# Weight sums of the seven-product networks: VectorE adds in place, or accumulating transfers into DRAM scratch

## The chip, the cores and the metric

The kernel runs on one core of one Trainium2 chip. The metric is the device time of one execution in microseconds; the time before is the median of three executions.

## What is computed

Two transformer blocks in a row on 512 tokens of width 1024, in float32. The parts that the change touches are the three feed-forward networks:

```
u = relu(rms_norm(h) @ mlp_w1);  h = h + (u * u) @ mlp_w2            # mlp: 1024 -> 4096 -> 1024
x = x + 0.5 * (silu(n @ w1) * (n @ w3)) @ w2                          # ffn1 and ffn2: 1024 -> 2816 -> 1024
```

Everything else (a mixer of forgetting attention and gated linear attention, cross attention to a memory of 256 rows, differential attention, a sparse attention, the projections) is as it was.

## The kernel before

Each float32 factor is split into a high and a low part, and a product is three matmuls (high by high, high by low, low by high). Weights come from DRAM into `raw` (two panels of 1024 rows by 256 columns, 1 MB each), ScalarE makes the high part (`wh`), VectorE the low part (`wl`), and TensorE multiplies. A panel p is loaded once `conv_done` says that panel p-2 has been converted; it is converted once TensorE has read panel p-2 out of `wh` and `wl`. The loads are issued in program order on SP's queue, whose waits stand in front of them.

Part of each network's first layer is done by seven products of half-size blocks in place of eight (a Winograd form of Strassen's scheme), in phases: three for mlp, two each for ffn1 and ffn2. A phase has groups: two for each mlp phase, four for each ffn phase, 22 groups in all. A group multiplies a 2 by 2 arrangement of 512x256 weight blocks, A11 and A12 (from `one`) and A21 and A22 (from `two`), with token blocks that are ready in SBUF. Its seven left factors are A11, A12, A22 and four sums: S3 = A11 + A21, S1 = A21 + A22, S2 = S3 + A22, S4 = A12 + S2 (the signs lie in the token blocks). A block's number of conversion is its place in A11, A12, A22, S3, S1, S2, S4. TensorE takes them as A11, A12, S2, S3, S1, A22, S4; from the second group on, S4 of the group before stands after A11 of the next (`in_turn`). Converted blocks go round six slots (`RING = 6`), so conversion n of a phase waits until product n-5 is done.

Four blocks are loaded for a group (`group_loads`, the transfer is L630), 512 KB each, into four buffers BP, BZ, BQ, BR. The buffers are those of `raw` or, for every other group, a spare area (`xl_f`, for ffn2 `al_f`). A11 lies in BP, A21 in BZ, A12 in BQ, A22 in BR. When VectorE has made the low part of A11, it adds in place (`add_up`, L3022): `sum_3` makes S3 in BP, `sum_1` makes S1 in BZ, `sum_2` makes S2 in BR after the low part of A22, `sum_4` makes S4 in BQ after the low part of A12. ScalarE's `block_high` (L2055) turns a block into its high part; for A11 it waits until all three of A11, A12 and A22 have landed. VectorE's `block_low` (its line in the profile is L2499, that of the helper `low`) makes the low part. ScalarE's `kept` (L2062) takes a product out of PSUM; TensorE's products S2, S1 and A22 wait for the first, second and third of a group. GpSimd has no work in the kernel.

Of the kernel before, what the change touches and what calls it, by code (L numbers as in the profile page):

```python
# [5 lines left out]
ALU = mybir.AluOpType  # L6
# [134 lines left out]


RING = 6
BP, BZ, BQ, BR = range(4)
BUF = {A11: BP, A12: BQ, A22: BR, S3: BP, S1: BZ, S2: BR, S4: BQ}
SUM = {S3: 1, S1: 2, S2: 3, S4: 4}


def net_of(g):
# [23 lines left out]
    return 12 * NETS.index(name) + 7 * PHASES[name, 1][0] + 3 * m + n  # L173


def sum_count(g, n):

    return 20 * (net_of(g) + 1) + 4 * g + n


def token_count(name, m, n):

    return 20 * NETS.index(name) + 4 * PHASES[name, 1][0] + 5 * m + n


def buffers(g):
# [89 lines left out]
def build(nc, d, out):  # L276
    ctx = ExitStack()
    with ctx:
# [118 lines left out]
        out_t, out_d = sem("out_t"), sem("out_d")  # L397
        out_c = [sem("out_c" + str(half)) for half in range(2)]
        st_z, st_r = ([sem(f"st_{b}{n}") for n in range(2)] for b in "zr")
        st_h, st_l, st_a, st_q, st_e, st_c = (sem("st_" + n) for n in ("h", "l", "a", "q", "e", "c"))  # L400


# [135 lines left out]
        def weights(g):  # L538
# [3 lines left out]
                return tuple(mw1[:, :, r * D + (2 * i + e) * PC:r * D + (2 * i + e + 1) * PC] for e in range(2))  # L542
            return tuple(w[:, :, (r - 1) * D + i * PC:(r - 1) * D + (i + 1) * PC] for w in ffw[net][0:2])

        def same_buffers(g):

            return [q for q in range(g) if buffers(q) == buffers(g)]
# [5 lines left out]
        def _(sp):  # L553
# [61 lines left out]
            def group_loads(g, p, free):  # L615

                one, two = weights(g)
                before = same_buffers(g)
                for b, src in ((BZ, two[:, 0:HT]), (BP, one[:, 0:HT]), (BQ, one[:, HT:KT]), (BR, two[:, HT:KT])):
                    if before:  # L620
                        q = before[-1]
                        if b in (BP, BR):
                            sp.wait_ge(st_a, sum_count(q, 3 if b == BP else 4))
                        else:
                            sp.wait_ge(st_l, high_count(q, S1 if b == BZ else S4))
                    if buffers(g):
# [3 lines left out]
                    sp.dma_start(raw_of(g, b), src).then_inc((st_r, st_z, st_r, st_r)[b][buffers(g)], 16)  # L630

            def phase(name, r, free, w2):

                g0, n, p = PHASES[name, r]
                for g in range(g0, g0 + n):
                    group_loads(g, p, free)
                last = g0 + n - 2
                for j in range(4):
                    if j == 0:
                        sp.wait_ge(st_l, high_count(last, S1))  # L640
                        sp.wait_ge(st_a, sum_count(last, 3))
# [82 lines left out]
            sp.wait_ge(out_d, 16 * QT)  # L724


        @block.tensor
# [854 lines left out]
        def _(act):  # L1582
# [885 lines left out]
        def _(dve):  # L2468
# [543 lines left out]
            def block_low(g, a):  # L3012

                dve.wait_ge(st_h, high_count(g, a))
                if a in SUM:
                    dve.wait_ge(st_a, sum_count(g, SUM[a]))
                to_h, to_l = parts_of(g, a)
                low(to_l, raw_of(g, BUF[a]), to_h, st_l)

            def add_up(g, to, of):  # L3020

                nc.vector.tensor_tensor(raw_of(g, to), raw_of(g, to), raw_of(g, of), ALU.add).then_inc(st_a, 1)  # L3022

            def sum_3(g):

                dve.wait_ge(st_l, high_count(g, A11))
                dve.wait_ge(st_z[buffers(g)], 16 * len(same_buffers(g)) + 16)
                add_up(g, BP, BZ)

            def sum_1(g):  # L3030

                dve.wait_ge(st_a, sum_count(g, 1))
                add_up(g, BZ, BR)

            def sum_2(g):

                dve.wait_ge(st_l, high_count(g, A22))
                dve.wait_ge(st_a, sum_count(g, 2))
                add_up(g, BR, BP)

            def sum_4(g):

                dve.wait_ge(st_l, high_count(g, A12))
                dve.wait_ge(st_a, sum_count(g, 3))
                add_up(g, BQ, BR)

            def bank(g, at):

# [20 lines left out]
            def first_blocks(g):  # L3069

                def early():
                    block_low(g, A11)
                    block_low(g, A12)

                def later():
                    block_low(g, A22)
                    sum_3(g)
                    sum_1(g)
                    block_low(g, S3)
                    sum_2(g)  # L3080
                return early, later, lambda: block_low(g, S1)

            def mlp_phase(r):

                g0, n, p = PHASES["mlp", r]

                def relu_square(g, buf, c, u):
                    dve.wait_ge(st_c, 3 * g + c)
                    nc.vector.scalar_tensor_tensor(buf, buf, 0.0, buf, ALU.max, ALU.mult).then_inc(ml_e, 1)

                def low_part(k, side, src, count):
                    dve.wait_ge(ml_hi, count)
                    low(al[:, k:k + 2, side], src, ah[:, k:k + 2, side], ml_lo)

                for g in range(g0, g0 + n):
                    k, more = 4 * (g - g0), g + 1 < g0 + n
                    block_low(g, S2)
                    sum_4(g)
# [24 lines left out]
                    relu_square(g, E_ul, 3, 2 * g + 2)  # L3123
                g, k = g0 + n - 1, 4 * (n - 1)
                low_part(k + 2, LEFT, E_ul, made_count(g, 3))
                low_part(k, RIGHT, E_tr, made_count(g, 4))
                conv(p + 1)

            def ffn_phase(name, r, dst):
# [17 lines left out]
                for g in range(g0, g0 + n):  # L3147
                    more = g + 1 < g0 + n
                    block_low(g, S2)
                    sum_4(g)  # L3150
# [5 lines left out]
                    if more:  # L3156
                        block_low(g + 1, A11)
                        block_low(g + 1, A12)
                        block_low(g + 1, A22)
                        sum_3(g + 1)  # L3160
                        sum_1(g + 1)
                    made_22(g)
                    if not more:
                        conv(p)
                    else:
                        block_low(g + 1, S3)
                        sum_2(g + 1)
# [510 lines left out]
```

## Time and profile before

| | |
|---|---|
| median of three executions | 2138.14 us (2136.89 to 2138.54) |
| the profiled execution, its own time | 2138.95 us |
| its span | 2137.2 us |
| TensorE (PE) busy | 2118.8 us, 99% of the span |
| VectorE (DVE) busy | 1372.5 us, 64% |
| ScalarE (ACT) busy | 1032.6 us, 48% |
| GpSimd (POOL) busy | 0.2 us |
| read from HBM, written | 188.73 MB, 2.10 MB |

The span is that of the profiled execution from its first to its last instruction; the 1.75 us around it belong to its own time. All starts are microseconds from the span's start. PE's busy time counts matmuls whose ends are modelled. SPq is SP's queue: its rows show when a transfer was issued, not when it landed.

### The profile page before, as it was taken

The numbers are of one execution on the slowest core, as the hardware profiler recorded it, in microseconds if no ns is written. First come the engines' busy times: TensorE is split into PE (matmuls) and PEld (weight loads), VectorE is DVE, ScalarE is ACT, GpSimd is POOL, SyncE is SP. The second block draws the span as 40 slices with busy tenths as digits, with TensorE's granted clock in tenths as the row PEclk, the third lists the DMA queues.
The fourth block names the chain that finished last, engine by engine and source line by source line (L and its number), as shares of the span: only waits on it lengthen the run. The fifth ranks groups of instructions, "written<-read, shape, count | busy, mean of one in ns | idle before, by whom it ended". The sixth has DMA issues, their size and how long they took to land.

```text
span 2137.2 us, 32530 instructions
## 1 busy us (share of the span) xinstructions
PE 2118.8 (99%) x13100; PEld 1819.8 (85%) x13100; DVE 1372.5 (64%) x2281; ACT 1032.6 (48%) x1738; POOL 0.2 (0%) x4
## 2 busy tenths in 40 slices
PE   9999999999999999999999999999999999999999
PEld 7888988888998988898988888887777888899997
DVE  4664663467664767775856777647776356686674
ACT  6654545543533543453543565546666234354344
POOL 0000000000000000000000000000000000000000
PEclk9999999999999999999999999999999999999999
DMA  5121522133233132424323622321111233242421
GB/s 189 60 80 60 180 97 80 40 99 118 80 119 118 61 98 84 138 75 138 100 80 98 181 83 82 98 84 50 40 37 40 79 99 99 87 139 72 138 68 71
DMA packets 190920, 199.74 MB, mean 93 GB/s; under 512 B 8481, under 2 KB 185778, under 8 KB 190258
## 3 DMA queue, kind: packets, MB, share of 16 engines
q1 hardware_dynamic: 190770, 197.66, 29.2%
q8 instruction: 104, 1.70, 0.3%
q14 instruction: 46, 0.38, 0.1%
HBM read 188.73 MB, written 2.10 MB: 89 GB/s over the span
## 4 chain that ended last, share of the span: by engine, by line
PE 93%; DVE 3%; ACT 2%; issue 1%; DMA 1%; SPq 0%; DVEq 0%; ACTq 0%
PE lin L733 20%; PE lin L735 19%; PE lin L734 19%; PE mix L1279 3%; PE mix L1280 3%; PE mix L1281 3%; PE score L1279 3%; PE score L1280 3%; PE score L1281 3%; PE turned L834 3%; PE score L929 3%; PE mix L943 2%; PE turned L1279 1%; PE turned L1280 1%; PE turned L1281 1%
## 5 line engine op out<-in xcount | busy, mean ns | idle before, releaser
L733 PE MATMUL lin<-xh,wh 128*128 128x512 f32 (+1 forms) x1032 | 407.5, 395 | 1.7 <-DVE wl L2494 1.2
L735 PE MATMUL lin<-xh,wl 128*128 128x512 f32 (+1 forms) x1032 | 394.8, 383 | 0.0
L734 PE MATMUL lin<-xl,wh 128*128 128x512 f32 (+1 forms) x1032 | 393.7, 382 | 0.0
L733 PE MATMUL lin<-ah,wh 128*128 128x512 f32 (+1 forms) x788 | 308.5, 392 | 1.4 <-DVE al L2499 0.6
L735 PE MATMUL lin<-ah,wl 128*128 128x512 f32 (+1 forms) x788 | 306.0, 388 | 0.0
L734 PE MATMUL lin<-al,wh 128*128 128x512 f32 (+1 forms) x788 | 305.9, 388 | 0.0
L2488 DVE TENSOR_TENSOR wl<-raw,wh 128x2048 fp32r<-128x2048 f32 x85 | 194.8, 2292 | 123.7 <-ACT wh L1595 123.7
L733 PEld LDWEIGHTS lin<-xh,wh 128*128 128x128 f32 x1032 | 194.2, 188 | 45.4 <-issue 9.6
L735 PEld LDWEIGHTS lin<-xh,wl 128*128 128x128 f32 x1032 | 194.0, 188 | 39.0
L734 PEld LDWEIGHTS lin<-xl,wh 128*128 128x128 f32 x1032 | 194.5, 188 | 34.8 <-issue 1.0
L1595 ACT ACTIVATE wh<-raw 128x2048 fp32r<-128x2048 f32 x85 | 162.0, 1906 | 113.4 <-PE lin L735 106.4
L733 PEld LDWEIGHTS lin<-ah,wh 128*128 128x128 f32 x788 | 148.0, 188 | 33.2 <-issue 1.6
L735 PEld LDWEIGHTS lin<-ah,wl 128*128 128x128 f32 x788 | 147.9, 188 | 30.7
L734 PEld LDWEIGHTS lin<-al,wh 128*128 128x128 f32 x788 | 148.0, 188 | 30.1 <-issue 0.2
L2494 DVE TENSOR_TENSOR wl<-raw,wh 128x1024 fp32r<-128x1024 f32 x90 | 109.5, 1220 | 40.4 <-ACT wh L1602 39.9
L2602 DVE CUSTOM_DVE_ANT_0 arena<-score,cst 128x128 f32<-128x128 f32 (+2 forms) x224 | 97.6, 486 | 58.0 <-PE score L929 46.6
L1692 ACT ACTIVATE arena<-arena,negm 128x128 f32<-128x128 f32 (+2 forms) x224 | 122.8, 555 | 3.1 <-DVE negm L2602 3.0
L1680 ACT ACTIVATE arena<-turned 128x512 f32<-128x512 f32 (+1 forms) x128 | 68.8, 582 | 112.5 <-PE turned L834 112.2
L1602 ACT ACTIVATE wh<-raw 128x1024 fp32r<-128x1024 f32 x90 | 94.1, 1052 | 36.1 <-PE lin L735 23.8
L1280 PE MATMUL mix<-arena_r,wh 128*128 128x256 f32 x352 | 98.9, 281 | 0.0
L1281 PE MATMUL mix<-arena_r,wl 128*128 128x256 f32 x352 | 98.9, 281 | 0.0
L1279 PE MATMUL mix<-arena_r,wh 128*128 128x256 f32 x352 | 98.9, 281 | 0.0
(434 smaller groups left out, 4301.1 us busy)
## 6 DMA issues: line engine op xcount, KB each, us to landing
raw<-in_w_in_dram SPq DMA_DIRECT2D x38, 1024.0 KB, 5.3
raw<-in_ffn_w_dram SPq DMA_DIRECT2D x28, 1024.0 KB, 5.2
raw<-in_mlp_w_dram SPq DMA_DIRECT2D x20, 1024.0 KB, 5.2
raw<-in_ffn_w_dram SPq DMA_DIRECT2D x32, 512.0 KB, 4.8
raw<-in_xattn_wkv_dram SPq DMA_DIRECT2D x8, 1024.0 KB, 5.3
raw<-in_w_out_dram SPq DMA_DIRECT2D x8, 1024.0 KB, 5.3
xl_f<-in_ffn_w_dram SPq DMA_DIRECT2D x16, 512.0 KB, 6.0
al_f<-in_ffn_w_dram SPq DMA_DIRECT2D x16, 512.0 KB, 5.5
```

The source lines that it names most:

```text
L733: nc.tensor.matmul(o, w[0], x[0], start=first, stop=False)
L734: nc.tensor.matmul(o, w[0], x[1], start=False, stop=False)
L735: return nc.tensor.matmul(o, w[1], x[0], start=False, stop=last)
L1279: nc.tensor.matmul(o[:, c, :], left_h[:, k, cols], XS_h[:, b, k, :], start=begins, stop=False, skip_group_check=True)
L1280: nc.tensor.matmul(o[:, c, :], left_h[:, k, cols], XS_l[:, b, k, :], start=False, stop=False, skip_group_check=True)
L1281: mm = nc.tensor.matmul(o[:, c, :], left_l[:, k, cols], XS_h[:, b, k, :], start=False, stop=k == HT - 1, skip_group_check=True)
L1595: nc.scalar.activation(wh[:, p % 2], raw[:, p % 2], ACT.Copy).then_inc(hi_done, 1)
L1602: nc.scalar.activation(wh[:, p % 2, :, cols], raw[:, p % 2, :, cols], ACT.Copy).then_inc(hi_half[c], 1)
L1692: op = nc.scalar.activation(PB[:, s % 2, a, col:col + nk], SM[:, a, col:col + nk], ACT.Exp, bias=negm[:, at:at + 1], scale=-1.0, accum_out ...
L2488: nc.vector.tensor_tensor(wl[:, p % 2], raw[:, p % 2], wh[:, p % 2].bitcast(F32), ALU.subtract).then_inc(conv_done, 1)
L2494: nc.vector.tensor_tensor(wl[:, p % 2, :, cols], raw[:, p % 2, :, cols], wh[:, p % 2, :, cols].bitcast(F32), ALU.subtract).then_inc(conv_d ...
L2602: op = nc.vector.tensor_tensor_reduce(out=SM[:, a, col:col + nk], in0=ps[a][:, col:col + nk], in1=mask, scale=scale, scalar=BIG, op0=ALU.a ...
```

## The change

The sums are no longer made on VectorE. GpSimd, idle until now, issues transfers from DRAM to DRAM: for each unit eight of them, each waiting for the one before (`su`). A unit is one group of mlp (blocks of 512x256, 512 KB a transfer, six units) or a whole phase of ffn1 or ffn2 (512x1024, 2 MB a transfer, four units). In a unit S3, S1, S2 and S4 are each made by a plain copy and an accumulating transfer (`accum_op=add`) onto it. It starts when TensorE has finished the first five panels.

SP now loads seven blocks for a group: A11, A12 and A22 first; then, once the unit's sums are there, S1 into BZ; S3 into BP when A11's low part is made; S2 into BR when A22's low part is made and S3 and S1 of the group have landed; S4 into BQ. ScalarE waits for the landing of a sum in place of the addition. The waits on `st_a` for sums go.

```diff
-SUM = {S3: 1, S1: 2, S2: 3, S4: 4}
+SUM = {S3: 0, S1: 1, S2: 2, S4: 3}
+UNITS = [(g_, 1, PC) if key_[0] == "mlp" else (g_, n_, n_ * PC) ...]
+        block_sums = [nc.dram_tensor(f"block_sums{u}", (4, HT * PART, width), F32, kind="Internal").ap() ...]
...
             def group_loads(g, p, free):
...
+                load(BP, one[:, 0:HT], st_r, S3, None)
+                load(BQ, one[:, HT:KT], st_r, S4, None)
+                load(BR, two[:, HT:KT], st_r, S2, None)
+                sp.wait_ge(su, 128 * (u + 1))
+                load(BZ, made(S1), st_z, S1, None)
+                load(BP, made(S3), st_z, None, A11)
+                sp.wait_ge(st_z[n], 64 * len(before) + 32)
+                load(BR, made(S2), st_z, None, A22)
+                load(BQ, made(S4), st_z, None, A12)
...
+        @block.gpsimd
+        def _(pool):
+            def step(n, dst, src, **kw):
+                if n:
+                    pool.wait_ge(su, 16 * n)
+                pool.dma_start(dst, src, **kw).then_inc(su, 16)
+            pool.wait_ge(lin_done, 2 * SUMS_FROM)
+            for u, (g, n, width) in enumerate(UNITS):
...
+                step(8 * u, s3, a11)
+                step(8 * u + 1, s3, a21, accum_op=ALU.add)
+                step(8 * u + 2, s1, a21)
+                step(8 * u + 3, s1, a22, accum_op=ALU.add)
+                step(8 * u + 4, s2, s3)
+                step(8 * u + 5, s2, a22, accum_op=ALU.add)
+                step(8 * u + 6, s4, s2)
+                step(8 * u + 7, s4, a12, accum_op=ALU.add)
...
-                    act.wait_ge(st_a, sum_count(g, SUM[a]))
+                    act.wait_ge(st_z[buffers(g)], 64 * len(same_buffers(g)) + (32 if a in (S1, S3) else 64))
...
-                        sum_3(g + 1)
-                        sum_1(g + 1)
...
-                        sum_2(g + 1)
```

The helper `load` in `group_loads` waits, in this order, for the buffer's last user in the group before that had the same buffers, for the low part of the block that the sum replaces, and for what the old code waited for (`conv_done` or `lin_done`), and then issues one transfer.

## Rows read from the trace of the kernel before

**Rows 1.** The page: busy times, and SP's DMA queue.

```profile
PE 2118.8 (99%) x13100; PEld 1819.8 (85%) x13100; DVE 1372.5 (64%) x2281; ACT 1032.6 (48%) x1738; POOL 0.2 (0%) x4
...
q1 hardware_dynamic: 190770, 197.66, 29.2%
```

**Rows 2.** Waits of PE: who waited for what: us in total, times, longest.

```profile
PE score L1279 <- DVE wl L2499: 1.2, 2, 0.8
```

**Rows 3.** Windows: busy us of each engine, clock, DMA share, GB/s.

```profile
240.00:320.00 80.00, 79.72 (x461) 70.40 (x460) 46.75 (x48) 34.46 (x48) 0.00 (x0) 1.00 0.43 145
...
540.00:580.00 40.00, 40.00 (x317) 39.00 (x315) 29.00 (x32) 23.59 (x31) 0.00 (x0) 1.00 0.21 70
```

**Rows 4.** Groups of instructions by line: VectorE's sums.

```profile
L3022 DVE TENSOR_TENSOR raw<-raw 128x1024 f32<-128x1024 f32 x44 | 53.7, 1219 | 0.4
...
L3022 DVE TENSOR_TENSOR xl_f<-xl_f 128x1024 f32<-128x1024 f32 x28 | 34.2, 1220 | 0.2
...
L3022 DVE TENSOR_TENSOR al_f<-al_f 128x1024 f32<-128x1024 f32 x16 | 19.5, 1220 | 0.1
```

**Rows 5.** First products of the mlp phases: min/median/max ns, first and last start.

```profile
L1279 PE MATMUL score<-arena_r,xh x24: 277/281/284, 534.4 to 556.9; 128*128 128x256 f32 x24
...
L1279 PE MATMUL score<-arena_r,wh x24: 277/281/283, 540.1 to 551.2; 128*128 128x256 f32 x24
...
L1279 PE MATMUL score<-arena_r,xh x24: 277/281/284, 617.9 to 640.3; 128*128 128x256 f32 x24
...
L1279 PE MATMUL score<-arena_r,xh x24: 277/281/284, 701.3 to 723.7; 128*128 128x256 f32 x24
```

**Rows 6.** DMA issues by line: KB each, median us to landing.

```profile
raw<-in_w_in_dram SPq DMA_DIRECT2D x38, 1024.0 KB, 5.3
...
raw<-in_ffn_w_dram SPq DMA_DIRECT2D x32, 512.0 KB, 4.8
```

**Rows 7.** L630, the block loads: landing in the window 510 to 523, and in all.

```profile
DMA to landing us min/median/max: 3.9/6.0/8.5
...
DMA to landing us min/median/max: 3.7/5.0/9.8
```

**Rows 8.** PE's timeline when panel 5 starts, and SP's where two networks' block loads start.

```profile
70.28 0.36 PE L733 MATMUL lin<-wh,xh 128*128 128x256 f32 x1
...
510.54 7.58 SPq L630 DMA_DIRECT2D raw<-in_mlp_w_dram  x4
...
864.10 9.08 SPq L630 DMA_DIRECT2D raw<-in_ffn_w_dram  x4
```

**Rows 9.** DVE's timeline, first mlp phase: low parts of A11 and A22.

```profile
524.35 1.22 DVE L2499 TENSOR_TENSOR xh<-raw,xh 128x1024 fp32r<-128x1024 f32 x1
...
529.79 1.22 DVE L2499 TENSOR_TENSOR wl<-raw,wh 128x1024 fp32r<-128x1024 f32 x1
```

**Rows 10.** ACT's timeline, same phase: A11 of the second group, then `kept`.

```profile
540.68 1.04 ACT L2055 ACTIVATE wh<-xl_f 128x1024 fp32r<-128x1024 f32 x1
542.66 0.63 ACT L2080 ACTIVATE arena<-arena 128x512 f32<-128x512 f32 x1 [0.94 <-DVE arena L3055]
...
543.87 0.58 ACT L2062 ACTIVATE arena<-score 128x512 f32<-128x512 f32 x1
```

**Rows 11.** Timelines of DVE, ACT and PE, first group of ffn1.

```profile
878.99 1.22 DVE L2499 TENSOR_TENSOR xh<-raw,xh 128x1024 fp32r<-128x1024 f32 x1 [2.26 <-ACT xh L2055]
...
887.79 1.06 ACT L2055 ACTIVATE wh<-raw 128x1024 fp32r<-128x1024 f32 x1 [1.21 <-DVE raw L3022]
...
890.67 0.39 PE L1279 MATMUL score<-arena_r,wh 128*128 128x256 f32 x1 [0.81 <-DVE wl L2499]
```

**Rows 12.** Second group of ffn1: DVE's low part of A11, ACT's high part of S2.

```profile
894.62 1.22 DVE L2499 TENSOR_TENSOR wl<-xl_f,wh 128x1024 fp32r<-128x1024 f32 x1
...
905.13 1.06 ACT L2055 ACTIVATE wh<-xl_f 128x1024 fp32r<-128x1024 f32 x1 [1.75 <-PE mix L1281]
```

**Rows 13.** ACT's timeline in the panels of the memory's keys and values.

```profile
234.85 1.06 ACT L1602 ACTIVATE wh<-raw 128x1024 fp32r<-128x1024 f32 x1 [2.98 <-DMA raw<-in_xattn_wkv_dram]
```

More of the change, by code:

```diff
@@ L143 @@
 RING = 6
+SUMS_FROM = P0["fv"]
 BP, BZ, BQ, BR = range(4)
 BUF = {A11: BP, A12: BQ, A22: BR, S3: BP, S1: BZ, S2: BR, S4: BQ}
-SUM = {S3: 1, S1: 2, S2: 3, S4: 4}
+SUM = {S3: 0, S1: 1, S2: 2, S4: 3}
+UNITS = [(g_, 1, PC) if key_[0] == "mlp" else (g_, n_, n_ * PC) for key_, (g0_, n_, _) in PHASES.items()
+         for g_ in range(g0_, g0_ + n_, 1 if key_[0] == "mlp" else n_)]
+UNIT_OF = {g_: u_ for u_, (g0_, n_, _) in enumerate(UNITS) for g_ in range(g0_, g0_ + n_)}
 def net_of(g):
@@ L173, in part_count @@
     return 12 * NETS.index(name) + 7 * PHASES[name, 1][0] + 3 * m + n
-def sum_count(g, n):
-    return 20 * (net_of(g) + 1) + 4 * g + n
 def token_count(name, m, n):
-    return 20 * NETS.index(name) + 4 * PHASES[name, 1][0] + 5 * m + n
+    return 20 * NETS.index(name) + 5 * m + n
 def buffers(g):
@@ L399, in build @@
         st_z, st_r = ([sem(f"st_{b}{n}") for n in range(2)] for b in "zr")
+        su = sem("su")
         st_h, st_l, st_a, st_q, st_e, st_c = (sem("st_" + n) for n in ("h", "l", "a", "q", "e", "c"))
@@ L543, in weights @@
             return tuple(w[:, :, (r - 1) * D + i * PC:(r - 1) * D + (i + 1) * PC] for w in ffw[net][0:2])
+        block_sums = [nc.dram_tensor(f"block_sums{u}", (4, HT * PART, width), F32, kind="Internal").ap() for u, (_, _, width) in enumerate(UNITS)]
         def same_buffers(g):
@@ L617, in group_loads, with load @@
                 one, two = weights(g)
[L618 to L626, printed above, removed]
+                before, n = same_buffers(g), buffers(g)
+                u = UNIT_OF[g]
+                at = (g - UNITS[u][0]) * PC
+                def load(b, src, signal, last, extracted):
+                    if last is not None and before:
+                        sp.wait_ge(st_l, high_count(before[-1], last))
+                    if extracted is not None:
+                        sp.wait_ge(st_l, high_count(g, extracted))
+                    if n:
                         sp.wait_ge(lin_done, 2 * free)
@@ L629, in group_loads, with made @@
                         sp.wait_ge(conv_done, p - 1 + b // 2)
-                    sp.dma_start(raw_of(g, b), src).then_inc((st_r, st_z, st_r, st_r)[b][buffers(g)], 16)
+                    sp.dma_start(raw_of(g, b), src).then_inc(signal[n], 16)
+                def made(a):
+                    return tiles(block_sums[u][SUM[a]])[:, :, at:at + PC]
+                load(BP, one[:, 0:HT], st_r, S3, None)
[7 more added lines that the diff above has]
+                load(BQ, made(S4), st_z, None, A12)
             def phase(name, r, free, w2):
@@ L640, in phase @@
                         sp.wait_ge(st_l, high_count(last, S1))
-                        sp.wait_ge(st_a, sum_count(last, 3))
                     elif j == 1:
@@ L724, in _ @@
             sp.wait_ge(out_d, 16 * QT)
+        @block.gpsimd
+        def _(pool):
+            def step(n, dst, src, **kw):
+                if n:
+                    pool.wait_ge(su, 16 * n)
+                pool.dma_start(dst, src, **kw).then_inc(su, 16)
+            pool.wait_ge(lin_done, 2 * SUMS_FROM)
+            for u, (g, n, width) in enumerate(UNITS):
+                (net, r), i = PHASE_OF[g]
+                if net == "mlp":
+                    at = r * D + 2 * i * PC
+                    a11, a12 = (mw1[:, ks, at:at + PC] for ks in (slice(0, HT), slice(HT, KT)))
+                    a21, a22 = (mw1[:, ks, at + PC:at + 2 * PC] for ks in (slice(0, HT), slice(HT, KT)))
+                else:
+                    (a11, a12), (a21, a22) = ([w[:, ks, (r - 1) * D:r * D] for ks in (slice(0, HT), slice(HT, KT))] for w in ffw[net][0:2])
+                s3, s1, s2, s4 = (tiles(block_sums[u][k]) for k in range(4))
+                step(8 * u, s3, a11)
[6 more added lines that the diff above has]
+                step(8 * u + 7, s4, a12, accum_op=ALU.add)
         @block.tensor
@@ L3014, in block_low @@
                 dve.wait_ge(st_h, high_count(g, a))
-                if a in SUM:
-                    dve.wait_ge(st_a, sum_count(g, SUM[a]))
                 to_h, to_l = parts_of(g, a)
                 low(to_l, raw_of(g, BUF[a]), to_h, st_l)
[L3020 to L3045, printed above, removed]
             def bank(g, at):
@@ L3076, in later @@
                     block_low(g, A22)
-                    sum_3(g)
-                    sum_1(g)
                     block_low(g, S3)
-                    sum_2(g)
                 return early, later, lambda: block_low(g, S1)
@@ L3097, in mlp_phase @@
                     block_low(g, S2)
-                    sum_4(g)
                     if g > g0:
@@ L3149, in ffn_phase @@
                     block_low(g, S2)
-                    sum_4(g)
                     if g > g0:
@@ L3159, in ffn_phase @@
                         block_low(g + 1, A22)
-                        sum_3(g + 1)
-                        sum_1(g + 1)
                     made_22(g)
@@ L3166, in ffn_phase @@
                         block_low(g + 1, S3)
-                        sum_2(g + 1)
                         block_low(g + 1, S1)
```

## The prediction

> **What bounds the kernel now.** I read the page first: TensorE is busy 2118.8 of 2137.2 us, the two converting engines 64% and 48%, and GpSimd does nothing [rows 1]. So work taken from VectorE is worth only the time that PE waits for VectorE. The windows put a place to that: in the first mlp phase PE is busy 40.00 of 40.00 us at the full clock [rows 3]. The waits of PE say the same: in all networks it waits for a converted block that the sums delay twice, 1.2 us in total, 0.8 the longest [rows 2]. The third view is the timelines of the first group of a phase and of the second, on every engine, for the slack of each block [rows 5, 9 to 12]; the last is the DMA views, since the change is mostly transfers [rows 1, 6, 7].
>
> The reader is to see a kernel that PE sets. A product of a group takes (540.1 - 534.4) / 2 = 2.85 us [rows 5], so a group 20 us; every deadline below is a product's start.
>
> **What is removed.** The 44 + 28 + 16 = 88 sums at 1.22 us are 107 us of VectorE [rows 4], beside a busy PE. They can give back at most the 1.2 us of [rows 2], and that only if S2 comes no later than now.
>
> **What a transfer costs.** SP's queue moved 197.66 MB in 190770 packets in 29.2% of 16 engines' span [rows 1]: 52 ns for 1036 bytes, 317 GB/s over 16 engines. 512 KB is 1.65 us of that. The shortest landing of such a block is 3.7 and 3.9 us [rows 7], take L = 3.8, so 2.2 us are fixed. That gives 5.5 us for 1 MB (the row has 5.3 [rows 6]), and 8.8 us for 2 MB.
>
> **The chain of sums on GpSimd.** No row shows an accumulating transfer or one from DRAM to DRAM. For the copies I take the same 3.8 and 8.8 us. An accumulate reads two streams and writes one. From below it costs what a copy does; from above I allow four times the data time. I take twice: 5.5 us and 15.4 us. The six mlp units are then 6 x 4 x (3.8 + 5.5) = 223 us, the four ffn units 4 x 4 x (8.8 + 15.4) = 387 us, together 610 us. They start when five panels are done, at 70 us [rows 8], and end at 680 us. By the lower bound they end at 70 + 48 x 3.8 + 32 x 8.8 = 534 us, by the upper (8.8 and 28.6 us for an accumulate) at 970 us. The first unit is wanted about 518 us and done after 37, and ffn1's first at 864 us [rows 8] is done at 70 + 223 + 97 = 390: SP's wait on `su` costs nothing.
>
> The Trainium skill (DMA: Bandwidth & Descriptors, Anatomy of one DMA) gives about 2.0 us plus the bytes over 436 GB/s for a transfer issued from GpSimd. By it the 48 small and 32 large steps would be some 154 + 218 = 372 us, an estimate from the page, and no traffic would be left when the networks begin. Its fixed part agrees with the 2.2 us above.
>
> **The new chain of loads, with idle DMA engines.** S3 and S2 are now two landings in a row behind A11's low part. In ffn1's first group that low part ends at 878.99 + 1.22 = 880.2; plus 2L is 887.8, and S2's high part starts at 887.79 today [rows 11]. No change. In the second group it ends at 895.84 [rows 12]. S2 of that group is product 9 of the phase and S2 of the first, product 2, starts at 890.67 [rows 11], so it is wanted at 910.6 and, with 1.06 + 1.22 us of conversion and 0.2 of handing over, landed by 908.1: 2L may be 12.2, and L 6.1. In the first group of an mlp phase A11's low part ends at 525.6 and A22's at 531.0 [rows 9]; S2 is issued at 531.1, lands at 534.9 and is wanted in SBUF by 540.1 - 2.5 = 537.6. So at L = 3.8 no product waits.
>
> **The queue on SP.** The next group's A11, A12 and A22 are now issued behind S2 and S4 of this one, and ScalarE's A11 waits for all three. In an mlp phase that is five blocks from 531.1: 2.2 + 5 x 1.65 = 10.5 us, 541.6. Behind the waiting A11 stands `kept`: A11's high part, two steps and `kept` itself are about 2.8 us [rows 10], and S1's product, the fifth, wants it at 534.4 + 4 x 2.85 = 545.8. So A11 must have landed by 543.0: 1.4 us to spare, no cost alone.
>
> **Beside GpSimd's transfers** it is no longer free. If the chain of sums runs until 680 us, it covers the mlp phases that start at 534.4 and 617.9, and not the third at 701.3 [rows 5]. Then its 2 MB steps move data (6.6 + 13.2) / 24.2 = 82% of the time. If the two queues share the engines evenly meanwhile, the loads go at 1 - 0.41 = 0.59 of their rate. The five blocks take 2.2 + 8.2 / 0.59 = 16.1 us, land at 547.2, and PE waits 4.2 us for `kept`. S2 of the first group has L = 5.0 on the mean and fits; entirely beside accumulates, at a third of the rate, L is 7.1 and S2 comes 2.3 us late; I take 1 us. That is 5 us a phase, 10 in two.
>
> The Trainium skill (DMA: Bandwidth & Descriptors, Queues, rings and completion order) says that an engine goes round its queues packet by packet, and that it doesn't matter which engine issued a transfer; that speaks for this sharing, and with GpSimd's 4 KB rows against SP's 1 KB rows for a worse one. No row of before shows two busy queues.
>
> Earlier, the memory's keys and values are the tightest place: eight panels of 1 MB in 5.7 us of PE each (48 matmuls of 256 columns at 2.85 / 24 us), DMA share 0.43 over that stretch [rows 3], and ScalarE waits 2.98 us for a load with PE still fed [rows 13]. Beside the mlp sums, which move data 53% of the time, the 3.3 us of a load become 4.5; four tight loads make up to 4.8 us, and I take 2 (bounds 0 and 8). Elsewhere a panel has twice the columns, so some 11 us of PE for the same load, and I take nothing. Sum: 10 + 2 = 12 us.
>
> **Rivals.**
> *Slower by shared DMA engines* (the forecast). For it: 48 x 0.52 + 32 x 2.1 = 92 MB written and more than that read, beside 200 MB today, and margins of 1.4 us. From 2 us (one phase touched lightly) up: if the sums run until 970 us they cover the three mlp phases and ffn1's first and perhaps second, and at a third of the rate the five blocks take 2.2 + 24.8 = 27 us, 15 too many, with 2.3 for S2; five times 17, plus 8, is 93 us.
>
> *The networks don't notice* (not slower). The chain of sums ends before 534 us, as it does if an accumulate costs a copy, or the engines serve both queues without loss. Then nothing waits: 2138 us, within 2 us. It decides at an end of the chain before 534 us, or at L under 5.4 us with A11 landing within 12 us. Against it: an accumulate must read twice. The skill's sum above would give this.
>
> *The sums are late.* SP waits on `su` in the networks, and everything behind it in SP's queue. For mlp that begins when a 512 KB step takes over (701 - 70) / 48 = 13.1 us on the mean. With 28 us for an accumulate and 3.8 for a copy the mean is 16, the last mlp unit comes at 838 in place of 701, and the time is some 137 us more, 2275 us; slower still is open above. Against it: 13.1 is over three times the landing of such a block.
>
> *Faster.* S2 comes earlier with VectorE free and both waits of [rows 2] go: 1.2 us, 2137 us, which a measurement can't tell. For more, VectorE would have to slow PE in a way that no wait shows.
>
> **How the numbers follow.** Contention slows it: 0.54, of which a tenth stays under 0.2%. Unnoticed: 0.27. Late: 0.13. Faster or a small other gain: 0.06, of which half is over 0.2%. About 0.2%, 4 us, is what a measurement of this kernel tells from no change. So slower 0.54 x 0.9 + 0.13 = 0.62, faster 0.03, the same the rest, 0.35. The sum stands against the profiled execution's 2138.95 us, 0.8 over the median: 2138 + 12 = 2150 us. The likeliest case alone has 2140 to 2231. The range takes in the unnoticed case below, 2136, and the heavier contention above and a mild lateness, to 2225; the rest of lateness and of gains stays out.
>
> **What would show it.** Right: rows L3022 gone; VectorE's busy time down by some 107 us; a queue of GpSimd with 80 transfers from 70 us on, ending near 680; PE waits at L1279, released by ACT `kept` (L2062) or by a low part, in the first two mlp phases and in neither of the later networks; landings of block loads over 5 us before the end of the sums and 3.8 after. Wrong: the chain of sums ending before 534 us with PE as busy as before in the phases; or SP waiting on `su` past 701 us, with idle stretches of PE of tens of us ahead of a phase. Waits in ffn2, where no sums run any more, would say that my 2L chain or the order of the queue was mis-sized, not the sharing.

## The result and the profile after

| | before | after |
|---|---|---|
| median | 2137.83 us | 2215.36 us (2212.23 to 2219.13) |
| ratio of the two, interval | | 1.0364 [1.0346, 1.0382] |
| span of the profiled execution | 2137.2 us | 2213.3 us |

The change costs some 77 us; 12 were forecast. The page of the changed kernel, against [rows 1] (its L1322 is L1279 of before, L2542 is L2499, L2105 is L2062, L633 is L630):

```profile
PE 2129.8 (96%) x13100; PEld 1829.4 (83%) x13100; DVE 1280.8 (58%) x2193; ACT 1028.8 (46%) x1738; POOL 81.1 (4%) x84
...
q1 hardware_dynamic: 225618, 232.27, 33.0%
q0 software_dynamic: 33024, 92.28, 17.7%
...
block_sums<-in_ffn_w_dram POOLq DMA_DIRECT2D x24, 2048.0 KB, 14.5
...
block_sums<-in_mlp_w_dram POOLq DMA_DIRECT2D x36, 512.0 KB, 6.8
block_sums<-block_sums POOLq DMA_DIRECT2D x8, 2048.0 KB, 10.2
```

VectorE has 88 instructions fewer and 91.7 us less to do, not the 107 of the prediction: that sum took each addition's whole duration, and in the rows of VectorE neighbouring instructions overlap by about 0.1 us at either end. (Without traffic, in experiment 12, it is 92.7 us, so the transfers have no part in it.) Of the last three rows the first two mix copies and accumulates. PE has as many matmuls as before, and yet is busy 11.0 us longer. Its waits, against [rows 2] (us in total, times, longest):

```profile
PE score L1322 <- DVE wl L2542: 46.0, 5, 16.6
PE mix L1322 <- DVE wl L2542: 16.1, 3, 7.7
...
PE lin L776 <- DVE wl L2531: 1.9, 1, 1.9
PE lin L776 <- DVE arena L2573: 1.7, 1, 1.7
```

The first two rows, 62.1 us where [rows 2] had 1.2, are the networks. PE's timeline puts them into the three mlp phases, 13.73 + 7.68, 13.79 + 6.54 and 16.55 + 1.90 = 60.2 us:

```profile
557.60 0.58 PE L1322 MATMUL score<-arena_r,wh 128*128 128x256 f32 x1 [13.73 <-DVE wl L2542]
...
587.72 0.58 PE L1322 MATMUL mix<-arena_r,wh 128*128 128x256 f32 x1 [7.68 <-DVE wl L2542]
...
667.77 0.58 PE L1322 MATMUL score<-arena_r,wh 128*128 128x256 f32 x1 [13.79 <-DVE wl L2542]
...
777.77 0.58 PE L1322 MATMUL score<-arena_r,wh 128*128 128x256 f32 x1 [16.55 <-DVE wl L2542]
```

The last two rows of the waits are the panels of the memory's keys and values, 3.6 us. So 76.1 us of span are some 61 of waits in the networks, some 3 in those panels, 11 of slower matmuls, and 1 spread elsewhere.

**Which load is late.** The chain that ended last, over the first mlp phase (start, length, what):

```profile
521.18 10.03 DMA raw<-in_mlp_w_dram
531.24 1.07 ACT xh L2098
532.33 1.24 DVE xh L2542
533.58 10.31 DMA raw<-block_sums
...
546.41 13.21 DMA xl_f<-in_mlp_w_dram
...
561.99 10.38 DMA xl_f<-block_sums
...
573.28 12.05 DMA xl_f<-block_sums
```

Read it downwards. A22 takes 10 us to land, and A11's conversion waits for it: A11's low part ends at 533.6, where it ended at 525.6 in the kernel before [rows 9]. PE itself is 3.6 us behind the kernel before at this point (its first product starts at 538.0, not 534.4 [rows 5]), so some 4 us are A22's. Then S3 is issued and takes 10.3 us; S2 is issued behind its landing, a chain that I call the join below. ScalarE's timeline gives the landings, 543.9 for S3 and 555.2 for S2:

```profile
543.92 1.06 ACT L2098 ACTIVATE xh<-raw 128x1024 fp32r<-128x1024 f32 x1 [9.73 <-DMA raw<-block_sums]
...
555.23 1.06 ACT L2098 ACTIVATE wh<-raw 128x1024 fp32r<-128x1024 f32 x1 [9.30 <-DMA raw<-block_sums]
```

So the two landings in a row are 533.6 to 555.2, 21.6 us where 2 x 3.8 were counted, and PE, out of products at 543.9, starts S2's at 557.6. The second group repeats it with S3 at 562.0 and S2 at 573.3.

**Why the landings are long.** Landings of the block loads in the window 500 to 800 us, against [rows 7], what GpSimd's queue moved meanwhile (packets, MB, share of 16 engines), and GpSimd's timeline:

```profile
DMA to landing us min/median/max: 3.9/10.7/15.5
...
q0 software_dynamic: 11308, 44.88, 59.4%
...
518.75 0.76 POOL L748 DMA_DIRECT2D block_sums<-block_sums  x1 [13.53 <-DMA block_sums<-in_ffn_w_dram]
528.18 1.24 POOL L748 DMA_DIRECT2D block_sums<-in_ffn_w_dram  x1 [8.67 <-DMA block_sums<-block_sums]
543.63 0.77 POOL L748 DMA_DIRECT2D block_sums<-block_sums  x1 [14.21 <-DMA block_sums<-in_ffn_w_dram]
...
775.24 1.25 POOL L748 DMA_DIRECT2D block_sums<-in_ffn_w_dram  x1 [11.02 <-DMA block_sums<-block_sums]
```

Here a 2 MB copy takes 9.4 us (518.8 to 528.2) and an accumulate 15.4 (528.2 to 543.6); from one issue to the next the medians of ffn's steps are 10.5 and 15.5 us, and those of mlp's 4.3 and 7.7. The last step begins at 775. SP's S3 of the chain above was issued at 533.6, in the middle of that accumulate. The DMA queues (packets, MB, share of 16 engines) in the windows 533.6 to 536.5, then 537 to 541, then 547 to 552:

```profile
q0 software_dynamic: 152, 0.62, 107.5%
...
q0 software_dynamic: 176, 0.72, 89.9%
q1 hardware_dynamic: 169, 0.17, 15.8%
...
q0 software_dynamic: 404, 1.65, 81.4%
q1 hardware_dynamic: 401, 0.39, 22.6%
```

In the first 2.9 us after the issue not one packet of SP's queue (q1) is recorded; the first starts at 537.1, 3.5 us after the issue. Part of that is there without any other traffic. In the kernel before a load issued at 537.43 has no packet in the 1.00 us from 537.43 to 538.43, and in the next 1.00 us:

```profile
q1 hardware_dynamic: 209, 0.21, 80.6%
```

So 1.0 us is usual and 2.5 us are added. It varies: of the changed kernel's SP loads between 500 and 800 us that were issued with no other load of SP in flight, eleven, the first packet came after 1.0 to 3.8 us, 3.5 in the median. After that the queues take turns, 176 to 169 and 404 to 401 packets, but one of GpSimd's has 4 KB and one of SP's 1 KB: between 547 and 552 us SP gets 0.39 of 2.04 MB, 19%, and 22.6 of the 104.0 points of engine time, 22%. This is turn by turn by packets, not an even share of time. The Trainium skill (DMA: Bandwidth & Descriptors, Queues, rings and completion order) has the engines go round their queues packet by packet; the second and third window agree (176 to 169 and 404 to 401 packets), the 2.5 us added at the start are not in that rule.

**The slower matmuls.** The windows 588 to 594 and 594 to 600 us (busy us and count of each engine, clock, DMA share, GB/s):

```profile
588.00:594.00 6.00, 6.00 (x31) 6.00 (x32) 3.14 (x4) 4.01 (x7) 0.00 (x0) 0.55 1.07 219
594.00:600.00 6.00, 6.00 (x53) 6.00 (x52) 1.57 (x3) 1.79 (x3) 0.00 (x0) 1.00 0.76 151
```

After the 7.68 us in which PE did nothing, the granted clock is 0.55, near its lower level of 1.2 GHz, and 31 matmuls fit into 6 us where 53 fit next. Each of the six waits in the mlp phases, the 1.90 us too, is followed by such a stretch of lower clock; in all the networks' matmuls are busy 11.5 us longer, the rest of PE's work 0.5 us shorter, which makes the 11.0.

### The profile page after: what moved, and what is told of

Same layout as the page of the kernel before. It is cut to its first block, busy times and chain, and to the rows that moved or that the text cites. A ratio compares the mean times of both kernels' runs of the same rounds, so it can differ in the third digit from the quotient of the medians.

```text
span 2213.3 us, 32502 instructions
## 1 busy us (share of the span) xinstructions
PE 2129.8 (96%) x13100; PEld 1829.4 (83%) x13100; DVE 1280.8 (58%) x2193; ACT 1028.8 (46%) x1738; POOL 81.1 (4%) x84
## 3 DMA queue, kind: packets, MB, share of 16 engines
q0 software_dynamic: 33024, 92.28, 17.7%
## 4 chain that ended last, share of the span: by engine, by line
PE 82%; DMA 10%; DVE 4%; ACT 3%; issue 1%; SPq 0%; DVEq 0%; ACTq 0%
PE lin L776 18%; PE lin L778 17%; PE lin L777 17%; PE mix L1322 3%; PE mix L1323 3%; PE mix L1324 3%; DMA xl_f<-block_sums 3%; PE turned L877 3%; PE score L972 3%; DMA raw<-block_sums 2%; PE score L1322 2%; PE mix L986 2%; PE score L1324 2%; PE score L1323 2%; DMA xl_f<-in_mlp_w_dram 2%; DMA raw<-in_mlp_w_dram 1%
## 5 line engine op out<-in xcount | busy, mean ns | idle before, releaser
L776 PEld LDWEIGHTS lin<-xh,wh 128*128 128x128 f32 x1032 | 194.2, 188 | 47.2 <-issue 11.5
L1322 PE MATMUL score<-arena_r,wh 128*128 128x256 f32 x296 | 86.4, 292 | 46.0 <-DVE wl L2542 46.0
L1322 PE MATMUL mix<-arena_r,wh 128*128 128x256 f32 x352 | 101.8, 289 | 16.1 <-DVE wl L2542 16.1
L1323 PE MATMUL mix<-arena_r,wh 128*128 128x256 f32 x352 | 101.3, 288 | 0.0
```

The lines of the kernel that those rows point to most:

```text
L776: nc.tensor.matmul(o, w[0], x[0], start=first, stop=False)
L1322: nc.tensor.matmul(o[:, c, :], left_h[:, k, cols], XS_h[:, b, k, :], start=begins, stop=False, skip_group_check=True)
L1323: nc.tensor.matmul(o[:, c, :], left_h[:, k, cols], XS_l[:, b, k, :], start=False, stop=False, skip_group_check=True)
```

## The experiments

The diffs are against the changed kernel, that of experiment 2 against the kernel before; `...` in a diff stands for lines left out. Ratios are to the kernel before.

**1. No traffic.** GpSimd's transfers go; the order of the loads stays. Weight blocks of the same size are loaded in place of the sums, so the kernel leaves the sums out.

```diff
-                    return tiles(block_sums[u][SUM[a]])[:, :, at:at + PC]
+                    return {S1: two[:, 0:HT], S3: two[:, 0:HT], S2: two[:, HT:KT], S4: one[:, HT:KT]}[a]
-                sp.wait_ge(su, 128 * (u + 1))
-        @block.gpsimd
-            ...
```

> The changed kernel without GpSimd's transfers: SP's seven loads of a group stand in their new order with their new waits, but the four sums are loaded straight from weight blocks of the same size (so the left factors are not the sums), and the wait on su is gone. Theory 1, the shared DMA engines stretch the landings: block loads land in about 3.8 to 5 us again, no wait of PE at L1322-like lines above 1 us, 2137 to 2141 us. Theory 2, the new order of the loads and the two landings in a row cost by themselves: at least 2180 us, with waits of several us in the mlp phases and in ffn1 and ffn2 alike.

2141.48 us, 1.0015 [1.0005, 1.0025]. Landings of block loads between 500 and 800 us:

```profile
DMA to landing us min/median/max: 3.6/4.9/10.1
...
891.21 0.39 PE L1293 MATMUL score<-arena_r,wh 128*128 128x256 f32 x1 [1.64 <-DVE wl L2513]
```

The mlp phases have no wait of PE for a block; PE's timeline shows 1.64 us in ffn1's first group and 1.80 in ffn2's. The traffic is needed for the loss, and the new order by itself costs 3.7 us.

**2. The kernel before, with the traffic for nothing.** GpSimd makes the sums in scratch, VectorE adds as before, nobody reads the scratch.

```diff
+        @block.gpsimd
+            ...  (the 80 steps; sums on VectorE and four loads a group kept)
```

> The kernel before, with its four early loads and the sums on VectorE, and GpSimd's 80 transfers beside it for nothing. Theory 1a, traffic costs only where loads stand late in a chain: 2142 to 2156 us, since A22's late landing (about 10 us in place of 5) still delays S2 by some us in each of three mlp phases. Theory 1b, traffic alone makes the whole loss: 2205 to 2220 us.

2143.30 us, 1.0030 [1.0018, 1.0041].

```profile
DMA to landing us min/median/max: 3.8/11.6/20.9
...
PE score L1313 <- DVE wl L2533: 2.9, 3, 1.7
...
PE lin L767 <- DVE wl L2522: 3.6, 2, 3.0
```

Its landings are as long as in the changed kernel (11.6 against 10.7 us), and it loses 5.5 us. Traffic alone 5.5, order alone 3.7, both 77: the loss comes of the two together, not of either. The old order loads four blocks ahead of any need; the new one issues the sums' loads only when low parts are made and puts two landings of the same group behind each other. Experiment 5 parts these two.

**3. Copies in place of accumulates.** The additions are left out, the steps and the bytes written stay.

```diff
-                step(8 * u + 1, s3, a21, accum_op=ALU.add)
+                step(8 * u + 1, s3, a21)
                 ...
```

> The changed kernel with every accumulating transfer made a plain copy (the sums are then only their last part). The bytes written stay the same, the second stream read goes. If an accumulate costs about twice a copy's data time, the chain of 80 steps ends near 600 us in place of 790, the third mlp phase and perhaps the second have no wait, and the time is 2160 to 2180 us. If accumulates cost what copies do, the chain ends near 790 us as before and the time stays 2210 to 2220 us.

2163.82 us, 1.0125 [1.0109, 1.0140]; q0 has 23808 packets for the same 92.28 MB written, and 12.4%. The accumulates thus bring packets of their own, 9216 of 33024, and 17.7% in place of 12.4% of the engines' span. The landings in the window 510 to 600 us, and GpSimd's last step:

```profile
DMA to landing us min/median/max: 3.8/9.9/14.6
...
628.37 0.74 POOL L748 DMA_DIRECT2D block_sums<-in_ffn_w_dram  x1 [9.17 <-DMA block_sums<-block_sums]
```

While copies of 2 MB run, a block lands in 9.9 us, almost as late as beside copies and accumulates in turn (10.6 in the same window of the changed kernel), and PE's waits in the first mlp phase are 17.4 us against 21.4. What falls is the time for which they run: the chain ends at 638 us in place of 793, the third mlp phase has no wait and the second one of 2.3 us. Most of the difference between 26 us and 77 is that.

**4. All units one group wide.** Steps of 512 KB with 1 KB rows everywhere, 176 steps.

```diff
-UNITS = [(g_, 1, PC) if key_[0] == "mlp" else (g_, n_, n_ * PC) ...]
+UNITS = [(g_, 1, PC) for g_ in range(GROUPS)]
             ...  (and ffn's source blocks a group wide)
```

> The changed kernel with every unit one group wide: ffn1's and ffn2's sums too are made in 512 KB transfers with rows of 1 KB, as many bytes in 176 steps. If the engines take turns packet by packet, the block loads of the mlp phases land in 6 to 8 us in place of 10 to 14 beside rows as short as their own, and PE's waits there fall from 20 us a phase to under 8; the chain runs longer, to about 1000 us, and puts small waits into ffn1: 2160 to 2190 us in all. If the queues share by bytes or time, landings stay at 10 to 14 us, ffn1's phases get waits of 20 us as well, and the time is 2230 us or more.

2162.45 us, 1.0119 [1.0095, 1.0143], landing median 6.4 us between 500 and 800 us; two thirds of the loss gone, although the chain of sums now ends at some 1200 us and touches ffn1, where the longest wait is 5.9 us. It changed three things at once, the rows, the amount of a step, and the length of the chain; 7, 9 and 14 vary the rows and the amount.

**5. S2 need not wait for S3's landing.** S2 and S4 are counted on semaphores of their own.

```diff
-                sp.wait_ge(st_z[n], 64 * len(before) + 32)
-                load(BR, made(S2), st_z, None, A22)
-                load(BQ, made(S4), st_z, None, A12)
+                load(BR, made(S2), st_y, None, A22)
+                load(BQ, made(S4), st_y, None, A12)
             ...  (ScalarE's waits likewise)
```

> The changed kernel with S2 and S4 counted on semaphores of their own, so that S2's load is issued when A22's low part is made and no longer waits until S3 has landed. If the two landings in a row (about 10 us each beside the sums) set the waits of the mlp phases, six groups lose up to 7 us each of their waits, PE keeps its clock for longer, and the time falls by 25 to 45 us, to 2170 to 2190 us. If only the throughput of the shared engines sets them, S3, S2 and what is behind them land when they did before, and the time is 2205 to 2217 us.

2186.76 us, 1.0227 [1.0211, 1.0242]: 28.6 of 77 us back. The other 48 need the traffic and the new order, but not the join. Between 505 and 800 us PE waits 32.1 us, 10.8 of them for `kept`, which the prediction had named:

```profile
560.90 0.55 PE L1322 MATMUL score<-arena_r,wh 128*128 128x256 f32 x1 [7.13 <-ACT arena L2105]
```

**6. The sums pause for mlp.** Nothing is transferred on GpSimd's queue during the mlp phases.

```diff
+PAUSED = {7: P0["ffn1"] - 1, 8: P0["mix2"]}
             ...
+                if u in PAUSED:
+                    pool.wait_ge(lin_done, 2 * PAUSED[u])
```

> The changed kernel with a pause in GpSimd's chain: ffn1's second unit is made from the start of ffn1 on and ffn2's two only when ffn1 is done, so that no sum is being made during an mlp phase. All 80 transfers remain. If it is their time beside the phases that costs, only what the order of the loads alone costs (3.7 us in the run without traffic) and a little of the panels' contention remain: 2140 to 2148 us. If the traffic costs wherever it is, or ffn1's second unit comes late, 2155 us or more.

2170.75 us, 1.0152 [1.0137, 1.0167], where 2140 to 2148 was expected. The mlp phases have no wait left, and their blocks land in 4.8 us in the median. But the two last units now run beside the first panels of the second block's mixer, and PE waits there:

```profile
1166.39 0.66 PE L779 MATMUL lin<-xh,wh 128*128 128x512 f32 x1 [2.63 <-DVE wl L2540]
...
1194.23 0.47 PE L1416 MATMUL score<-wl,ah 128*62 128x256 f32 x1 [2.31 <-DVE wl L2540]
1201.53 0.80 PE L779 MATMUL lin<-xh,wh 128*128 128x512 f32 x1 [3.85 <-DVE wl L2540]
```

**7. The ffn sums in steps of 512 KB, rows of 4 KB kept.** Each step is still waited for before the next. (SP's count of `su` is changed to match.)

```diff
-                if n:
-                    pool.wait_ge(su, 16 * n)
-                pool.dma_start(dst, src, **kw).then_inc(su, 16)
+                for q in range(4) if n >= 48 else (slice(0, 4),):
+                    if made[0]:
+                        pool.wait_ge(su, 16 * made[0])
+                    pool.dma_start(dst[:, q], src[:, q], **kw).then_inc(su, 16)
+                    made[0] += 1
             ...
```

> The changed kernel with ffn's sums made in 512 KB transfers, as in the run with narrow rows, but with rows of 4 KB as before; each transfer waits for the one before. If turns are taken packet by packet, so that the length of GpSimd's rows sets how long an SP packet waits, block loads in the mlp phases still land in 9 us or more and PE waits 10 us a phase or more, 2185 us or more in all. If it was the smaller transfers with their pauses that helped in the run with narrow rows, the landings and waits are as there, and the time is 2150 to 2168 us.

2157.75 us, 1.0106 [1.0081, 1.0131]:

```profile
DMA to landing us min/median/max: 3.6/6.3/12.3
...
q0 software_dynamic: 5845, 26.22, 39.3%
...
PE score L1327 <- DVE wl L2547: 6.3, 5, 3.8
```

A miss for the theory that long rows are the fault. With the same 4 KB rows and a quarter of a step, it is as good as experiment 4.

**8. Experiments 5 and 6 together.**

```diff
+PAUSED = {7: P0["ffn1"] - 1, 8: P0["mix2"]}
-                sp.wait_ge(st_z[n], 64 * len(before) + 32)
             ...
```

> The pause and the separate counts together, the best version with sums in DRAM that the theory of shared engines and landings in a row gives: ffn1's and ffn2's first groups no longer wait 1.6 us for S2 behind S3, so 2 to 4 us under the paused version, 2138 to 2143 us, and not faster than the kernel before by more than 1 us, since PE was busy all the time in those phases. If VectorE's sums had slowed PE in a way that no wait shows, this version would be at 2130 us or less.

2171.08 us, 1.0151 [1.0136, 1.0166]; 2138 to 2143 was expected. What experiment 6 loses is in mix2's panels, which the order of the block loads doesn't touch.

**9. Rows of 1 KB in steps of 1 MB.** The scratch holds each group's columns together. The memory set aside for GpSimd's descriptors is larger too (`dynamic_dma_scratch_size` 2560 in place of 2048).

```diff
-        block_sums = [... (4, HT * PART, width) ...]
+        block_sums = [... (4, width // PC, HT * PART, PC) ...]
...
+                for gs in (slice(0, 2), slice(2, 4)) if n >= 48 else (slice(0, 1),):
             ...
```

> The changed kernel with ffn's scratch laid out so that its transfers have rows of 1 KB, in steps of 1 MB (64 rows for each engine and step; the 512 KB steps of two earlier runs had 32 rows of 1 KB or 8 of 4 KB, the changed kernel's 2 MB have 32 of 4 KB). If packets of the two queues alternate one to one, a 512 KB block has 32 packets on an engine and can be held up by 32 accumulating packets of some 100 ns, 3.3 us, however large the transfer: block loads in the mlp phases land in about 5 to 7 us, PE waits there under 3 us a phase, and the time is 2150 to 2170 us. If a larger transfer holds the engines for as long as it lasts, waits lie between those of the changed kernel and of the 512 KB steps, 8 us a phase or more, and the time is 2180 us or more.

2181.84 us, 1.0222 [1.0200, 1.0245]:

```profile
DMA to landing us min/median/max: 3.6/7.1/13.6
...
PE score L1327 <- DVE wl L2547: 21.1, 5, 8.4
```

Expected was 2150 to 2170 if taking turns with long packets is all of it. With packets as short as SP's own it still loses 44 us, more than 4 KB rows in smaller steps. Only part of that is in the mlp phases, where PE waits 15.8 us (3.6 in experiment 7); the chain of sums runs until 977 us, into ffn1, and brings waits of 8.4 and 2.4 us there.

**10. The sums where the loads have slack.** The unit of ffn1's second phase is made between the phases of mlp and ffn1 (from 777.6 us), the two of ffn2 beside the second block's gated linear attention (from 1510.8 us).

```diff
+PAUSED = {7: P0["ffn1"] - 1, 8: P["ga1"]}
```

> As the paused version, but ffn2's two units are made late in the second block's attention, where the kernel before moves 30 to 50 GB/s, in place of its first panels. If the paused version's remaining loss was the contention in those first panels, it goes: 2140 to 2148 us. If it is the traffic wherever it lies, the time stays at 2165 to 2175 us.

2143.57 us, 1.0028 [1.0017, 1.0039], 71.8 us better than the change: all 80 transfers are still made, none beside an mlp phase or the second block's first panels. The mlp sums still run beside the panels of the memory's keys and values, where PE waits 2.6 us.

**11. Experiments 7, 5 and 10 together.**

> The quiet placement, 512 KB steps and separate counts for S2 and S4 together, the best version that the theory gives: 2137 to 2142 us, level with the kernel before, since VectorE's freed time is worth nothing where TensorE is always busy. If VectorE's sums had slowed TensorE anywhere, it would be 2130 us or less.

2154.68 us, 1.0084 [1.0069, 1.0099], where 2137 to 2142 was expected. Four times as many steps, each waiting for the one before, are a longer chain; it runs into ffn1, whose second unit is still being made until some 975 us, and PE waits:

```profile
902.39 0.58 PE L1330 MATMUL score<-arena_r,wh 128*128 128x256 f32 x1 [4.59 <-DVE wl L2550]
```

**12. Experiments 1 and 5 together: the order without the join, no traffic.** As in experiment 1 the sums are left out.

> The version without GpSimd's transfers (block loads of the same size in place of the sums), and with separate counts for S2 and S4. If the 3.7 us that the order of the loads cost there come from S2 standing behind S3's landing in ffn1's and ffn2's first groups, they shrink to 0 to 2 us: 2137 to 2140 us. If they come from other places, it stays at 2141 to 2142 us.

2138.41 us, 1.0004 [0.9995, 1.0013]. The 3.7 us of experiment 1 were, within 0.6, S2 behind S3. It also says what the removed sums are worth: nothing that can be measured, with VectorE relieved and no traffic to pay.

**13. Experiments 10 and 5 together.**

> The quiet placement with 2 MB steps, and separate counts for S2 and S4. The quiet version measured 5.7 us over the kernel before, the order's own share without traffic 3.3 us, which the separate counts took away. If the two add up, 2139 to 2142 us. If the separate counts do nothing here, as in the paused version, 2142 to 2146 us.

2142.71 us, 1.0022 [1.0013, 1.0031]. What remains is in the memory's keys and values, where the mlp sums run:

```profile
242.04 0.36 PE L779 MATMUL lin<-xh,wh 128*128 128x256 f32 x1 [1.50 <-DVE arena L2576]
...
271.36 0.77 PE L779 MATMUL lin<-ah,wh 128*128 128x512 f32 x1 [3.17 <-DVE wl L2534]
```

**14. Steps of 512 KB, four issued together.** Experiment 7 with one wait for four transfers, so the amount in GpSimd's queue is 2 MB again.

```diff
-                    if made[0]:
+                    if made[0] and q in (0, slice(0, 4)):
                         pool.wait_ge(su, 16 * made[0])
```

> The version with ffn's sums in 512 KB steps of 4 KB rows (2158 us), but with four such transfers issued together and then one wait, so that 2 MB stand in GpSimd's queue at once, as in the changed kernel. If it is the amount in the queue at once that delays SP's blocks (they start late and then alternate with as many packets), landings in the mlp phases return to about 10 us and the time to 2200 us or more. If it is the size of a single transfer, or the number of its rows for each engine, that matters, landings stay near 6 to 7 us and the time under 2170 us.

2202.99 us (2183.46 to 2211.17), 1.0296 [1.0244, 1.0349]:

```profile
DMA to landing us min/median/max: 3.6/10.0/19.1
...
PE score L1327 <- DVE wl L2547: 23.5, 4, 11.2
...
PE score L1327 <- ACT arena L2110: 13.1, 3, 8.9
```

Same transfers, same rows, one wait in four: the landings are back at 10 us. Side by side, in the window 500 to 800 us, with the share of the engines' time that GpSimd's queue took there (and PE's waits for converted blocks and `kept`, from 505 us on):

| | in GpSimd's queue at once | rows | its share | median landing | PE waits | time |
|---|---|---|---|---|---|---|
| changed kernel | 2 MB | 4 KB | 59.4% | 10.7 us | 58.3 us | 2215 us |
| 14 | 4 x 512 KB | 4 KB | 57.0% | 10.0 | 40.0 | 2203 |
| 9 | 1 MB | 1 KB | 48.5% | 7.1 | 15.8 | 2182 |
| 7 | 512 KB | 4 KB | 39.3% | 6.3 | 3.6 | 2158 |
| 4 | 512 KB | 1 KB | 39.7% | 6.4 | 5.2 | 2162 |
| 1 | nothing | | 0 | 4.9 | 0 | 2141 |

The length of a row changes nothing that can be seen at 512 KB. The landing goes with the amount in the queue, but the queue's share of the engines falls in step with it: with less in the queue there are more pauses between steps, and fewer bytes are moved meanwhile (26.2 MB in experiment 7, 44.9 in the changed kernel). No run holds one and changes the other, so which of the two sets the landing is open. (The times hold more than the landings, as the chains of sums end between 793 and some 1200 us.)

## Why the prediction was right in kind and wrong in size

- *PE sets the time, and the removed sums are worth at most 1.2 us.* Right: experiment 12 has 2138.41 us without them, 1.0004 [0.9995, 1.0013].
- *Price of the steps.* A 2 MB accumulate was 15.5 us in the median, 15.4 taken, a 2 MB copy 10.5 in place of 8.8. Mlp's copies and accumulates took 4.3 and 7.7 us in place of 3.8 and 5.5. So mlp's 48 steps took 301 us (69.5 to 370.8) and not 223, ffn's 32 took 422 and not 387, and the chain ended at 793 us, not 680, inside the bounds of 534 and 970. It covered the third mlp phase too, which has 18.45 of the 60.2 us, where none were counted. The cheaper sum set beside it, 372 us with no traffic left when the networks begin, is about half of the 723 us that the 80 steps took.
- *The wait on `su` is free.* Right; the late sums did not occur.
- *The order costs nothing alone.* Off by 3.7 us, in the first groups of ffn1 and ffn2 (experiments 1 and 12), where [rows 11] left it no slack and I took L = 3.8, the shortest landing, though [rows 7] has a median of 5.0. The waits are 1.64 + 1.80 us where [rows 2] has 1.2, and the clock is lower for 3.4 us behind the second.
- *Sharing.* This is the step that failed: "If the two queues share the engines evenly meanwhile, the loads go at 1 - 0.41 = 0.59 of their rate", and with it "S2 of the first group has L = 5.0 on the mean and fits" and the 1 us taken for it. Measured on the chain of the first mlp phase are landings of 10.0 to 13.2 us, above even the 7.1 that I had worked out for a load entirely beside accumulates. Of S3's 10.3 us, 3.5 passed before its first packet, and then SP had 22% of the engines' time, not a half or a third. I had named turns by packets as the worse case and put no number to it. With L = 10.3 my own rule of 2L gives what happened: 533.6 + 21 = 554.6 for S2, 555.2 in the trace, and PE had run dry at 543.9. The rule was right and its input was not. A second input was off as well: I let the rule start from A11's low part at its old time, and A22's late landing had put that off by some 4 us. In the two phases that I had counted as covered, 10 us became 41.7.
- *Who is late.* I put 4.2 of 5 us on `kept` behind the burst of five and 1 on S2. In the changed kernel it was S2 in every mlp phase. `kept` appears when the join is taken away (10.8 us in experiment 5), and with it in experiment 14 (13.1 us).
- *The memory's keys and values.* 2 us taken, 3.6 measured, inside its bounds.
- *Left out.* The waits cost again in the clock of the matmuls behind them: 11.0 us, a seventh of the loss.

Sized with what was measured, the sum is 60 in the mlp phases, 2 in ffn1 and ffn2, 3 in the panels and 11 of clock: 76 us, the difference of the spans. That the loss needs both the traffic and the new order is shown (1, 2, 12): either alone costs under 6 us. The join is 28.6 us of it (5). The other 48 us are not taken apart by any run; they are argued to lie in loads that are issued only when a low part is made, with the next group's behind them, since the old order bears the same landings (2). That less in GpSimd's queue at once shortens the landings is shown (7, 9, 14), but not whether by the amount or by the smaller share of the engines that goes with it. Why SP's queue gets its first packet 2.5 us later than usual is open: it may be that packets already handed to the engines go first, but no run looks inside.

None of the versions beats the kernel before. The best that keeps the sums in DRAM, experiment 13, is 4.2 us behind it.

## What to carry to other kernels

Read a transfer's cost to others from the landings of their loads while it is in flight, not from its bytes: background transfers of 2 MB made the median landing of a 512 KB block twice as long (10.7 against 4.9 us), and that cost 5.5 us where loads are issued ahead (experiment 2), 48 where they are issued just before their use (experiment 5), and 77 where one of them also waits for another's landing. If bulk transfers must run in the background, keep little of them in the queue at once (6.3 us a landing in experiment 7) and, which gave more, start them where the loads have slack (experiment 10). Work taken from an engine that nobody waits for is worth nothing, whatever its microseconds.

## What the runs showed of the hardware

- A DRAM to DRAM copy of 2 MB issued by GpSimd took 10.5 us in the median from its issue to the next, an accumulating one 15.5; of 512 KB, 4.3 and 7.7. Accumulates brought the queue's packets from 23808 to 33024 for the same 92.28 MB written.
- With both queues busy, packets alternated one to one (404 to 401) though one queue's had 4 KB and the other's 1 KB. A load's first packet came 1.0 us after its issue with the engines idle, and 1.0 to 3.8 us after it beside the sums (median 3.5).
- While 2 MB copies ran, a block landed in 9.9 us in the median; beside copies and accumulates in turn in 10.6 (510 to 600 us).
- Four transfers of 512 KB issued together delayed SP's blocks about as one of 2 MB did (10.0 and 10.7 us), and one at a time did much less (6.3; 4.9 beside nothing).
- PE's clock was granted at 0.55 in the 6 us after a wait of 7.68 us, then at 1.00.
